# Three attention stages of a two-block transformer: the search for row maxima spread over more steps, the softmax sums taken as columns, the division moved behind the transposition, one more addition per block on GpSimd

## The chip, the cores and the metric

One NeuronCore of a Trainium2 chip runs the whole program. The time is device microseconds from start to end of one execution; the runs of the kernel before have a median of 5038.33 us (5033.85 to 5042.69, three runs). Engines are named as the profile names them: PE is TensorE, PEld its weight load, DVE VectorE, ACT ScalarE, POOL GpSimd, SP SyncE; a "q" behind a name is the engine's queue (its semaphore and DMA instructions).

## The reference, cut to what matters

Two transformer blocks on 1024 tokens of width 1024: an MLA plus dilated attention block with 16 experts, then two layers that each have three kinds of attention on 1024 tokens plus 256 context tokens. The change touches those attentions that see every key:

```python
def mla_attention(q, k, v):                       # first block, 8 heads, 1024 keys
    s = jnp.einsum('bqhd,bkhd->bhqk', q_blk, k).astype(jnp.float32) * scale
    p = jax.nn.softmax(s, axis=-1).astype(v.dtype)
    return jnp.einsum('bhqk,bkhd->bqhd', p, v)

def diff_attend(q, k, v, lam):                    # each layer of the second, 8 maps, 1280 keys
    s = jnp.einsum('bqhmd,bkhmd->bhmqk', q, k).astype(jnp.float32) * (q.shape[-1] ** -0.5)
    p = jax.nn.softmax(s, axis=-1)

def gqa_attend(q, k, v):                          # each layer of the second, 6 heads, 1280 keys
    s = jnp.einsum('bqhgd,bkhd->bhgqk', qg, k).astype(jnp.float32) * (d ** -0.5)
    p = jax.nn.softmax(s, axis=-1).astype(v.dtype)
    o = jnp.einsum('bhgqk,bkhd->bqhgd', p, v)
```

So each needs, for every query, the maximum of its scores, the exponentials, their sum, their product with v, and a division.

## The kernel before, in words

All five such attentions go through one function, `stage_turned`: `am` (MLA, 8 heads in 4 pairs, 1024 keys), and in each of two layers `aa` (8 maps in 4 pairs, 1280 keys) and `ab` (6 heads in 3 pairs, 1280 keys). The profile writes no layer number, so `aa` and `ab` stand for both layers; the time tells them apart (layer 0 from 2560 us, layer 1 from 4110 us).

A pair of heads is cut in *blocks* of 512 queries (two in each pair; layer 0 has a third, small one of 256 context queries against 256 keys). A block is walked in *steps* of 128 keys, numbered i in the block and g in the stage: 8 steps in `am`, 10 in `aa` and `ab`, 2 in the small block. In a step

- PE (`scores`) multiplies 128 keys by 512 queries for both heads into the scores' PSUM buffers `sp`, two in turn; the scores come out turned, with keys on the partitions. A score takes one pass for a head in `aa`, two in `ab`, three in `am`.
- ACT (`exponentials`) writes exp of both heads, 128x1024, into a ring `pT` of six. The maximum is subtracted inside the matmul: a row of the operand `qA` (`qB` in `ab`) holds the negated maxima.
- PE (`values`), in odd steps only, multiplies two earlier steps' exponentials by v into `po`, eight passes of 512 columns in all.
- For the sums, the exponentials are added over the steps: DVE adds steps 0 and 1 and the block's last one into `accd`, POOL the steps between into `accp`, and DVE adds the two (L1535, L1540, POOL L1587).

The maxima of a block must be known before its first step, so they are *searched* while the block ahead of it runs. A *piece* is a matmul of 128 queries by up to 512 keys (`search`, L1396) into one of two PSUM buffers `mp`, and a DVE reduction of it to one column (L1519). A block has 16 pieces in `am` (2 heads x 4 tiles x 2), and 24 in `aa` and `ab` (2 x 4 x 3; of three pieces one is 256 wide). Each piece waits until the one two before it is reduced (semaphore `mc`). PE and DVE take them in the same order, four to a step: steps 0 to 3 in `am`, 0 to 5 in `aa` and `ab` (0 to 6 in a first block of layer 0, which also searches for the small one).

When all are reduced, `row` turns the maxima on PE (L1404), ACT copies them (L1478), and SP writes them to memory and reads them back as a row of the next block's operand (L1362, L1366); the next block's first scores wait for that (semaphore `rw`). It stands two steps behind the last searched one.

Behind a block's end, counted in steps from its last: 4 steps later PE sums over the partitions with a matrix of ones (`sums`, L1437, out 64x512 for each head) into a buffer of `mp`, in turn with the pieces; DVE takes the reciprocal of 128x512 (L1546) and multiplies `po` by it (L1551). 6 steps later PE turns the result (`turned`, L1446), behind the values, into a buffer of `sp`; ACT copies it out (L1495) and POOL stores it.

Every engine runs its own list in program order, with no reordering: an engine that waits for one semaphore holds up all that stands behind it. Inside one step DVE's list is: the pieces of the step, then `add(g - 2)`, then the normalisation; PE's is: scores, pieces, in odd steps sums and values, then `turned`, then `row`.

## Time and profile before

| | |
|---|---|
| median of the runs shown | 5038.33 us (5033.85 to 5042.69) |
| profiled execution, its own time | 5035.54 us |
| its span, from the first to the last instruction | 5033.9 us |
| granted TensorE clock over the span | 0.851 |
| the five stages (507 to 787, 2560 to 2890, 2935 to 3195, 4110 to 4425, 4460 to 4700 us) | 1425 us in all |

What lies around the span is 1.6 us, so times inside the span add straight to the time. The granted clock is 1.00 at 2.4 GHz and 0.50 at 1.2 GHz; a figure between is a mean over a stretch.

### The profile page before, as it was taken

Reading aid. Unit: us, or ns where it says so; the run is one execution under the profiler, and the core shown is the slowest. Engines: PE = TensorE matmul, PEld = TensorE weight load, DVE = VectorE, ACT = ScalarE, POOL = GpSimd, SP = SyncE. Lnnn points to the kernel's source line nnn. Section 1 sums busy time; section 2 is a strip of 40 time slices with the busy share of each in tenths; the row PEclk is TensorE's granted clock in tenths of the full one; section 3 lists DMA queues with packets and bytes.
Section 4 is the critical chain, followed back from the end, with each engine's and each line's share of the span. In section 5 each row is a group of like instructions: output and inputs, shape, how many; then the busy total and the mean of one; then the engine's idle time right before and its main releaser. Section 6 shows DMA issues by size and latency. Waiting matters only on the chain. (4 is left out here: it accounts for less than half of the span.)

```text
span 5033.9 us, 55601 instructions
## 1 busy us (share of the span) xinstructions
PE 3815.4 (76%) x18714; PEld 2694.3 (54%) x18714; DVE 2606.4 (52%) x4549; ACT 1773.2 (35%) x2670; POOL 1407.2 (28%) x974
## 2 busy tenths in 40 slices
PE   3985886886299995589968868576688978858557
PEld 3973444665278884477833334355576753324346
DVE  2114453432678786744445546466556535545465
ACT  1225224731077774422212312354422212312352
POOL 0213231000056662144613413200044613423102
PEclk6997798997699997799967868888799977868798
DMA  5228213316699994322232032423222331131333
GB/s 210 97 107 243 66 38 72 102 47 237 167 396 398 394 394 175 102 88 92 97 90 52 9 77 47 92 82 109 81 97 76 102 78 59 26 71 40 88 105 90
DMA packets 327678, 628.00 MB, mean 125 GB/s; under 512 B 115338, under 2 KB 171892, under 8 KB 326364
## 3 DMA queue, kind: packets, MB, share of 16 engines
q1 hardware_dynamic: 289080, 494.92, 31.4%
q0 software_dynamic: 34240, 113.67, 7.1%
q10 hardware_dynamic: 4068, 15.79, 0.8%
q8 instruction: 152, 2.49, 0.2%
q14 instruction: 138, 1.13, 0.1%
HBM read 485.18 MB, written 139.11 MB: 124 GB/s over the span
## 5 line engine op out<-in xcount | busy, mean ns | idle before, releaser
L2282 PE MATMUL pr_ps<-pr_wH,hT_part 128*128 128x512 f32 x1120 | 447.5, 400 | 0.0
L2052 ACT ACTIVATE ex_high<-ex_ring 128x2048 fp32r<-128x2048 f32 x192 | 368.7, 1920 | 96.0 <-PE ex_pg L2028 37.6
L2098 DVE TENSOR_TENSOR ex_ring_part<-ex_ring,ex_high 128x2048 fp32r<-128x2048 f32 x144 | 371.8, 2582 | 50.7 <-ACTq L2053 38.8
L2282 PE MATMUL pr_ps<-pr_wH,x_sb_part 128*128 128x512 f32 x896 | 366.2, 409 | 22.8 <-DVEq L2355 22.8
L2282 PE MATMUL pr_ps<-pr_w_part,x_sb_part 128*128 128x512 f32 x896 | 358.9, 401 | 0.0
L1519 DVE TENSOR_REDUCE aa_part<-aa_mp 128x1 f32<-128x512 f32 (+1 forms) x400 | 238.1, 595 | 207.1 <-PE aa_mp L1396 171.8
L1993 POOL TENSOR_TENSOR ex_ring_part<-ex_ring,ex_high 128x2048 fp32r<-128x2048 f32 x48 | 239.4, 4988 | 215.3 <-ACTq L2053 215.3
L1396 PE MATMUL aa_mp<-aa_kA,aa_qA 96*128 96x512 f32 (+1 forms) x400 | 199.0, 538 | 120.9 <-DVEq L1520 73.7
L1487 ACT ACTIVATE aa_pT<-aa_sp 128x1024 f32<-128x1024 f32 (+1 forms) x168 | 168.6, 1003 | 313.1 <-PE aa_sp L1417 304.1
L1519 DVE TENSOR_REDUCE ab_part<-ab_mp 128x1 f32<-128x512 f32 (+1 forms) x300 | 178.7, 596 | 182.8 <-PE ab_mp L1396 155.6
L2282 PEld LDWEIGHTS pr_ps<-pr_wH,hT_part 128*128 128x128 f32 x1120 | 217.2, 194 | 47.5
L2428 POOL TENSOR_TENSOR pr_w_part<-pr_w,pr_wH 128x512 fp32r<-128x512 f32 x96 | 124.4, 1296 | 406.8 <-ACTq L2308 405.2
L1396 PE MATMUL ab_mp<-ab_kA,ab_qA 128*128 128x512 f32 (+1 forms) x300 | 141.9, 515 | 120.1 <-DMA ab_v<-proj 57.1
L1658 PE MATMUL o_ps<-o_wH,o_yT 128*128 128x512 f32 x832 | 231.5, 396 | 0.0
L1587 POOL TENSOR_TENSOR aa_accp<-aa_accp,aa_pT 128x1024 f32<-128x1024 f32 x80 | 194.3, 2429 | 94.0 <-ACTq L1488 91.1
L1487 ACT ACTIVATE ab_pT<-ab_sp 128x1024 f32<-128x1024 f32 (+1 forms) x126 | 126.4, 1003 | 255.2 <-PE ab_sp L1417 250.8
L1396 PEld LDWEIGHTS aa_mp<-aa_kA,aa_qA 96*128 96x128 f32 x400 | 94.0, 236 | 226.2 <-DVEq L1520 170.5
L1428 PE MATMUL aa_po<-aa_pT,aa_v 128*64 128x512 f32 x672 | 213.2, 769 | 0.0
L2282 PEld LDWEIGHTS pr_ps<-pr_wH,x_sb_part 128*128 128x128 f32 x896 | 175.3, 196 | 58.5 <-issue 23.4
L2368 DVE TENSOR_REDUCE pr_ss<-pr_sqr 128x8 f32<-128x512 f32 (+2 forms) x80 | 49.6, 619 | 287.8 <-ACTq L2331 284.1
L1045 PE MATMUL ac_ps<-ac_kT,ac_qT 128*128 128x384 f32 (+1 forms) x204 | 75.4, 374 | 155.8 <-DVEq L1111 84.2
L2282 PEld LDWEIGHTS pr_ps<-pr_w_part,x_sb_part 128*128 128x128 f32 x896 | 174.7, 195 | 34.9
(387 smaller groups left out, 9026.5 us busy)
## 6 DMA issues: line engine op xcount, KB each, us to landing
ex_ring<-in_w_gate SPq DMA_DIRECT2D x64, 1024.0 KB, 9.6
ex_ring<-in_w_up SPq DMA_DIRECT2D x64, 1024.0 KB, 8.1
ex_ring<-in_w_down SPq DMA_DIRECT2D x64, 1024.0 KB, 7.9
z_d<-pr_zT POOLq DMA_DIRECT2D x120, 256.0 KB, 3.0
rt_mw<-in_w_ada SPq DMA_DIRECT2D x14, 2048.0 KB, 15.6
pr_w<-in_w_in SPq DMA_DIRECT2D x14, 2048.0 KB, 8.5
mod_w<-in_w_ada SPq DMA_DIRECT2D x10, 2048.0 KB, 13.1
proj<-pr_raw POOLq DMA_DIRECT2D x60, 256.0 KB, 2.3
```

The costliest lines, as they stand in the source:

```text
L1045: mm = tensor.matmul(ps[h % SB][:, at:at + m], q.bitcast(F32R), kk.bitcast(F32R), start=i == 0, stop=i == len(ab) - 1)
L1396: tensor.matmul(mp[:, k_ % 2, 0:w], qA[rows, b, j, q0:q0 + P].bitcast(F32R), kA[rows, b, j, a_:a_ + w].bitcast(F32R), start=True, stop=Tru ...
L1428: mm = tensor.matmul(po[j * dv:(j + 1) * dv, B % 2, 0:qn], v[:, p % 2, k0 // P + i, j * dv:(j + 1) * dv], pT[:, g % RP, j, 0:qn], start=i ...
L1487: scalar.activation(pT[:, g % RP, :, 0:qn], sp_[:, s % 2, :, 0:qn], ACT.Exp)
L1519: vector.tensor_reduce(part[:, B % 2, j * n + t, x:x + 1], mp[:, k_ % 2, 0:w], AX.X, ALU.max)
L1587: pool.tensor_tensor(acc, pT[:, (g - 3) % RP, :, 0:qn] if i == 3 else acc, pT[:, (g - 2) % RP, :, 0:qn], ALU.add).then_inc(ap_, 1)
L1658: mm = tensor.matmul(ps[:, t % 2, cols], yT[:, t % 2, part, c, :].bitcast(F32R), w[:, c, cols].bitcast(F32R), start=c == 0 and i == 0, sto ...
L1993: pool.tensor_tensor(w_part[:, c % SL].bitcast(F32R), w_sb[:, c % SL], wH[:, c % HL], ALU.subtract)\
L2052: scalar.activation(wH[:, c % HL].bitcast(F32R), w_sb[:, c % SL], ACT.Copy)
L2098: vector.tensor_tensor(w_part[:, c % SL].bitcast(F32R), w_sb[:, c % SL], wH[:, c % HL], ALU.subtract)
L2282: mm = tensor.matmul(ps[:, g % 4, :], x.bitcast(F32R), w[:, c % 2, kk, :].bitcast(F32R), start=kk == 0 and i == 0, stop=kk == KC - 1 and i ...
L2428: pool.tensor_tensor(w_part[w].bitcast(F32R), w_sb[w], wH[w], ALU.subtract).then_inc(w_low, 1)
```

## The change

The search of a block is spread evenly over all but the last two steps of the block ahead of it (`searched`): 3 pieces in each of 8 steps in layer 1 (4 and 3 in turn in a first block of layer 0), and 3, 3, 2, 3, 3, 2 in `am`. The row of maxima comes one step behind the last searched step instead of two (`row_at`).

POOL adds every step from the third to the last; DVE adds only the first two and then the two sums. DVE's additions stand three steps behind instead of two (`add(g - 3)`).

The sums come out as columns: `sums` uses 128 columns of `accd` as weights and one column of ones as the moving operand, eight matmuls for a block of 512 queries, and leaves 128x8 in `mp`. DVE takes the reciprocal of these eight columns. ACT copies `po` to `oT` undivided (`gathered`, 3 steps behind the end). PE turns it into a buffer of `mp` instead of one of `sp`, ahead of the values, and DVE divides while it copies out (`divided`). `slot_out` and `slot_den` now both count places among the pieces.

```diff
@@ -1235,26 +1235,22 @@
             p, B, blk, i = where(g)
             if size[blk] <= 2:
                 return []
-            ahead = [B + 1] if blk + 1 < NB and size[blk + 1] > 2 else [b for b in (B + 1, B + 2) if b % NB == 0 or size[b % NB] <= 2]
-            if blk == 0 and NB == 3:
-                ahead = [B + 1, B + 2]
-            if blk == 1 and NB == 3:
-                ahead = [B + 2]
+            ahead = [B + 1] if NB == 2 else [B + 1, B + 2] if blk == 0 else [B + 2]
             pcs = [(b, m) for b in ahead if b < NBLK for m in range(len(maxima(b)))]
-            return pcs[4 * i:4 * i + 4]
+            n = size[blk] - 2
+            return pcs[-(-len(pcs) * i // n):-(-len(pcs) * (i + 1) // n)] if i < n else []
 
         def row_at(B):
 
             if B == 0:
                 return -1
-            return 2 + max(g for g in range(TOT) if any(b == B for b, _ in searched(g)))
+            return 1 + max(g for g in range(TOT) if any(b == B for b, _ in searched(g)))
...
-        D_AT, F_AT, S_AT = 4, 6, 8
-        out_at = {end(B) + F_AT: B for B in range(NBLK)}
+        O_AT, D_AT, F_AT, S_AT = 3, 4, 6, 8
...
         def on_dve(blk, i):
-            return size[blk] <= 2 or i in (0, 1, size[blk] - 1)
+            return i < 2
...
@@ -1433,37 +1429,39 @@
                     qn, k_ = blocks[B % NB][1], slot_den(B)
                     pe.wait_ge(ac, B + 1)
                     pe.wait_ge(mc, k_ - 1)
-                    for j in range(2):
-                        mm = tensor.matmul(mp[j * dv:(j + 1) * dv, k_ % 2, 0:qn], ones[:, j * dv:(j + 1) * dv],
-                                           accd[:, B % 2, j, 0:qn], start=True, stop=True)
+                    for t in range(qn // P):
+                        for j in range(2):
+                            mm = tensor.matmul(mp[:, k_ % 2, 2 * t + j:2 * t + j + 1], accd[:, B % 2, j, t * P:(t + 1) * P],
+                                               ones[:, 0:1], start=True, stop=True)
                     mm.then_inc(mf, 1)
 
                 def turned(B):
-                    s = slot_out(B)
+                    k_ = slot_out(B)
                     pe.wait_ge(nr, B + 1)
-                    pe.wait_ge(sr, s - 1)
+                    pe.wait_ge(mc, k_ - 1)
                     for t in range(tiles_of(B)):
-                        mm = tensor.transpose(sp_[:, s % 2, 0, t * P:(t + 1) * P], oT[:, B % 2, t * P:(t + 1) * P], ident[:, :])
-                    mm.then_inc(st, 1)
+                        mm = tensor.transpose(mp[:, k_ % 2, t * P:(t + 1) * P], oT[:, B % 2, t * P:(t + 1) * P], ident[:, :])
+                    mm.then_inc(mf, 1)
 
                 pe.wait_ge(ones_in, 1)
                 for m in range(len(maxima(0))):
                     search(0, m, m)
                 row(0)
-                for g in range(TOT + F_AT):
+                for g in range(TOT + F_AT + 1):
                     if g < TOT:
                         scores(g)
                         for x, (B, m) in enumerate(searched(g)):
                             search(B, m, pieces_before[g] + x)
+                    for B in range(NBLK):
+                        if end(B) + D_AT == g:
+                            sums(B)
+                    for B in range(NBLK):
+                        if end(B) + F_AT == g:
+                            turned(B)
                     if g % 2:
-                        for B in range(NBLK):
-                            if end(B) + D_AT == g:
-                                sums(B)
                         for x in (g - 3, g - 2):
                             if 0 <= x < TOT:
                                 values(x)
-                    if g in out_at:
-                        turned(out_at[g])
                     for B in range(1, NBLK):
                         if rows_at[B] == g:
                             row(B)
@@ -1487,20 +1485,21 @@
                     scalar.activation(pT[:, g % RP, :, 0:qn], sp_[:, s % 2, :, 0:qn], ACT.Exp)
                     act.drain().then_inc(sr, 1)
 
-                def finished(B):
-                    s, n = slot_out(B), tiles_of(B)
-                    act.wait_ge(st, s + 1)
+                def gathered(B):
+                    qn = blocks[B % NB][1]
+                    act.wait_ge(pv, end(B) + 1)
                     if B >= 2:
-                        act.wait_ge(os_[B % 2], 16 * (B // 2))
-                    scalar.activation(o[:, B % 2, 0:n, :], sp_[:, s % 2, 0, 0:n * P].rearrange("p (t d) -> p t d", d=P), ACT.Copy)
-                    act.drain().then_inc(sr, 1)
+                        act.wait_ge(mf, slot_out(B - 2) + 1)
+                    scalar.activation(oT[:, B % 2, 0:qn], po[:, B % 2, 0:qn], ACT.Copy)
+                    act.drain().then_inc(nr, 1)
 
                 row(0)
-                for g in range(TOT + F_AT):
+                for g in range(TOT + F_AT + 1):
                     if g < TOT:
                         exponentials(g)
-                    if g in out_at:
-                        finished(out_at[g])
+                    for B in range(NBLK):
+                        if end(B) + O_AT == g:
+                            gathered(B)
                     for B in range(1, NBLK):
                         if rows_at[B] == g:
                             row(B)
@@ -1528,28 +1527,35 @@
                 def add(g):
                     p, B, blk, i = where(g)
                     qn, n = blocks[blk][1], size[blk]
+                    if i == n - 1 and n > 2:
+                        last = added(g)
+                        dve.wait_ge(*last)
+                        vector.tensor_tensor(accd[:, B % 2, :, 0:qn], accd[:, B % 2, :, 0:qn], accp[:, B % 2, :, 0:qn], ALU.add)
+                        dve.drain().then_inc(ac, 1)
                     if not on_dve(blk, i) or i == 0:
                         return
                     acc = accd[:, B % 2, :, 0:qn]
                     dve.wait_ge(sr, slot_scores(g) + 1)
                     vector.tensor_tensor(acc, pT[:, (g - 1) % RP, :, 0:qn] if i == 1 else acc, pT[:, g % RP, :, 0:qn], ALU.add)
                     dve.drain().then_inc(ad, 1)
-                    if i == n - 1:
-                        if n > 2:
-                            dve.wait_ge(ap_, p * pool_adds[NSTEP] + pool_adds[g % NSTEP])
-                            vector.tensor_tensor(acc, acc, accp[:, B % 2, :, 0:qn], ALU.add)
+                    if n == 2:
                         dve.drain().then_inc(ac, 1)
 
-                def normalised(B):
-                    qn, k_ = blocks[B % NB][1], slot_den(B)
+                def sums(B):
+                    n, k_ = 2 * tiles_of(B), slot_den(B)
                     dve.wait_ge(mf, k_ + 1)
-                    vector.reciprocal(rB[:, 0:qn], mp[:, k_ % 2, 0:qn])
+                    vector.reciprocal(rd[:, B % 2, 0:n], mp[:, k_ % 2, 0:n])
                     dve.drain().then_inc(mc, 1)
-                    dve.wait_ge(pv, end(B) + 1)
+
+                def divided(B):
+                    n, k_ = 2 * tiles_of(B), slot_out(B)
+                    dve.wait_ge(mf, k_ + 1)
                     if B >= 2:
-                        dve.wait_ge(st, slot_out(B - 2) + 1)
-                    vector.tensor_tensor(oT[:, B % 2, 0:qn], po[:, B % 2, 0:qn], rB[:, 0:qn], ALU.mult)
-                    dve.drain().then_inc(nr, 1)
+                        dve.wait_ge(os_[B % 2], 16 * (B // 2))
+                    vector.tensor_tensor(o[:, B % 2, 0:n // 2, :].rearrange("p t (j d) -> p (t j) d", d=dv),
+                                         mp[:, k_ % 2, 0:n * dv].rearrange("p (c d) -> p c d", d=dv),
+                                         rd[:, B % 2, 0:n].rearrange("p (c o) -> p c o", o=1).to_broadcast([P, n, dv]), ALU.mult)
+                    dve.drain().then_inc(mc, 1)
...
@@ -1561,15 +1567,18 @@
                 dve.drain().then_inc(ones_in, 1)
                 for m in range(len(maxima(0))):
                     search(0, m, m)
-                for g in range(TOT + F_AT):
+                for g in range(TOT + F_AT + 1):
                     if g < TOT:
                         for x, (B, m) in enumerate(searched(g)):
                             search(B, m, pieces_before[g] + x)
-                    if 0 <= g - 2 < TOT:
-                        add(g - 2)
+                    if 0 <= g - 3 < TOT:
+                        add(g - 3)
                     for B in range(NBLK):
                         if end(B) + D_AT == g:
-                            normalised(B)
+                            sums(B)
+                    for B in range(NBLK):
+                        if end(B) + F_AT == g:
+                            divided(B)
 
             @block.gpsimd
             def _(pool):
...
-                            pool.wait_ge(sr, slot_out(B) + 1)
+                            pool.wait_ge(mc, slot_out(B) + 1)
```

Three places in the engines' lists, from one block in the middle of stage `aa`, second layer. First DVE. Before, one block of ten steps; the x8 are the pieces of two steps, `nm` is the final maximum:

```order
L1519 TENSOR_REDUCE aa_part<-aa_mp 128x1 x8
L1535 TENSOR_TENSOR aa_accd<-aa_accd,aa_pT 128x1024
L1540 TENSOR_TENSOR aa_accd<-aa_accd,aa_accp 128x1024
L1519 TENSOR_REDUCE aa_part<-aa_mp 128x1 x8
L1535 TENSOR_TENSOR aa_accd<-aa_pT 128x1024
L1546 RECIPROCAL aa_rB<-aa_mp 128x512
L1551 TENSOR_TENSOR aa_oT<-aa_po,aa_rB 128x512
L1519 TENSOR_REDUCE aa_part<-aa_mp 128x1 x8
L1524 TENSOR_REDUCE aa_nm<-aa_part 128x8
```

The same block now:

```order
L1518 TENSOR_REDUCE aa_part<-aa_mp 128x1 x9
L1533 TENSOR_TENSOR aa_accd<-aa_accd,aa_accp 128x1024
L1518 TENSOR_REDUCE aa_part<-aa_mp 128x1 x3
L1547 RECIPROCAL aa_rd<-aa_mp 128x8
L1518 TENSOR_REDUCE aa_part<-aa_mp 128x1 x3
L1539 TENSOR_TENSOR aa_accd<-aa_pT 128x1024
L1518 TENSOR_REDUCE aa_part<-aa_mp 128x1 x3
L1555 TENSOR_TENSOR aa_o<-aa_mp,aa_rd 128x512
L1518 TENSOR_REDUCE aa_part<-aa_mp 128x1 x6
L1523 TENSOR_REDUCE aa_nm<-aa_part 128x8
```

Before, both additions stood behind the pieces of an odd step. Now each stands behind the pieces of an even step (i = 2 and i = 4), ahead of those of the odd step that follows.

Second PE, steps 3 to 5 of the block (`mp` from `kA` is a piece, `po` the values). Before:

```order
L1437 MATMUL aa_mp<-aa_accd,aa_one 64x512 x2
L1428 MATMUL aa_po<-aa_pT,aa_v 64x512 x4
L1417 MATMUL aa_sp<-aa_qA,aa_kA 128x512 x2
L1396 MATMUL aa_mp<-aa_kA,aa_qA 128x512
L1396 MATMUL aa_mp<-aa_kA,aa_qA 128x256
L1396 MATMUL aa_mp<-aa_kA,aa_qA 128x512 x2
L1417 MATMUL aa_sp<-aa_qA,aa_kA 128x512 x2
L1396 MATMUL aa_mp<-aa_kA,aa_qA 128x256
L1396 MATMUL aa_mp<-aa_kA,aa_qA 128x512 x2
L1396 MATMUL aa_mp<-aa_kA,aa_qA 128x256
L1428 MATMUL aa_po<-aa_pT,aa_v 64x512 x4
L1446 MATMUL aa_sp<-ident,aa_oT 128x128 x4
```

Now:

```order
L1434 MATMUL aa_mp<-aa_one,aa_accd 128x1 x8
L1424 MATMUL aa_po<-aa_pT,aa_v 64x512 x4
L1413 MATMUL aa_sp<-aa_qA,aa_kA 128x512 x2
L1392 MATMUL aa_mp<-aa_kA,aa_qA 128x512 x2
L1392 MATMUL aa_mp<-aa_kA,aa_qA 128x256
L1413 MATMUL aa_sp<-aa_qA,aa_kA 128x512 x2
L1392 MATMUL aa_mp<-aa_kA,aa_qA 128x512 x2
L1392 MATMUL aa_mp<-aa_kA,aa_qA 128x256
L1443 MATMUL aa_mp<-ident,aa_oT 128x128 x4
L1424 MATMUL aa_po<-aa_pT,aa_v 64x512 x4
```

Six pieces instead of eight stand between two groups of values, the turning moved ahead of the values and into `mp`, and the sums are eight matmuls of one column.

Third PE, the last steps of the block (the `nm` row is `row`, and the block's last values come just ahead of the next block's scores). Before:

```order
L1417 MATMUL aa_sp<-aa_qA,aa_kA 128x512 x4
L1428 MATMUL aa_po<-aa_pT,aa_v 64x512 x4
L1404 MATMUL aa_sp<-ident,aa_nm 8x128
L1417 MATMUL aa_sp<-aa_qA,aa_kA 128x512 x4
L1428 MATMUL aa_po<-aa_pT,aa_v 64x512 x4
```

Now:

```order
L1424 MATMUL aa_po<-aa_pT,aa_v 64x512 x4
L1413 MATMUL aa_sp<-aa_qA,aa_kA 128x512 x2
L1400 MATMUL aa_sp<-ident,aa_nm 8x128
L1413 MATMUL aa_sp<-aa_qA,aa_kA 128x512 x2
L1424 MATMUL aa_po<-aa_pT,aa_v 64x512 x4
```

The row of maxima moved one step nearer to the scores that wait for it, from ahead of step 8's scores to behind them.

## Rows read from the trace of the kernel before

**Rows 1.** The page: busy us of each engine, share of the span, instructions.

```profile
PE 3815.4 (76%) x18714; PEld 2694.3 (54%) x18714; DVE 2606.4 (52%) x4549; ACT 1773.2 (35%) x2670; POOL 1407.2 (28%) x974
```

**Rows 2.** Windows: length, busy of PE, PEld, DVE, ACT, POOL; clock, DMA share, GB/s.

```profile
563.10:758.20 195.10, 167.02 (x631) 87.98 (x630) 116.01 (x134) 54.34 (x61) 60.91 (x30) 0.97 0.20 47
4166.70:4394.50 227.80, 195.62 (x559) 76.50 (x559) 135.55 (x181) 66.60 (x73) 87.80 (x42) 0.79 0.13 29
4511.50:4667.60 156.10, 134.36 (x454) 63.97 (x453) 90.84 (x121) 44.41 (x49) 59.82 (x29) 0.87 0.16 34
2614.80:2862.80 248.00, 206.55 (x628) 85.28 (x628) 150.97 (x205) 72.14 (x85) 94.28 (x45) 0.78 0.13 30
2991.80:3161.10 169.30, 140.18 (x507) 69.05 (x506) 105.02 (x138) 48.05 (x57) 61.15 (x30) 0.89 0.16 36
```

**Rows 3.** PE's waits, 4110 to 4425: us in total, times, longest.

```profile
PE aa_mp L1396 <- DVEq L1520: 31.0, 70, 1.3
```

**Rows 4.** Timeline of steps 0 and 1 of an `aa` block, layer 1.

```profile
4281.31 0.73 PE L1417 MATMUL aa_sp<-aa_qA,aa_kA 97*128 97x512 f32 x2 [0.59 <-DMA aa_qA<-aa_nmd]
...
4282.32 5.82 DVE L1519 TENSOR_REDUCE aa_part<-aa_mp 128x1 f32<-128x512 f32 x8 [10.90 <-PE aa_mp L1396]
4283.09 0.39 PE L1396 MATMUL aa_mp<-aa_kA,aa_qA 96*128 96x256 f32 x1 [0.58 <-DVEq L1520]
...
4287.21 3.39 PE L1428 MATMUL aa_po<-aa_pT,aa_v 128*64 128x512 f32 x8
...
4290.53 0.73 PE L1417 MATMUL aa_sp<-aa_qA,aa_kA 97*128 97x512 f32 x2
```

**Rows 5.** Windows of 3.4 us in these steps (columns as in Rows 2).

```profile
4283.40:4286.80 3.40, 2.37 (x8) 1.24 (x7) 2.81 (x6) 1.02 (x1) 0.08 (x1) 0.99 0.00 0
4286.80:4290.20 3.40, 3.40 (x9) 0.76 (x8) 3.04 (x4) 0.00 (x0) 0.00 (x0) 0.50 0.01 2
```

**Rows 6.** Groups of DVE instructions by form, 4110 to 4425.

```profile
L1519 DVE TENSOR_REDUCE aa_part<-aa_mp 128x1 f32<-128x512 f32 x124 | 85.7, 692 | 97.2 <-PE aa_mp L1396 86.8
L1546 DVE RECIPROCAL aa_rB<-aa_mp 128x512 f32<-128x512 f32 x8 | 26.9, 3357 | 2.9 <-PE aa_mp L1437 2.1
L1519 DVE TENSOR_REDUCE aa_part<-aa_mp 128x1 f32<-128x256 f32 x62 | 26.3, 424 | 11.5 <-PE aa_mp L1396 5.5
```

**Rows 7.** Timeline: a block's first scores and first reduction, `am` then `ab`.

```profile
659.85 0.50 PE L1417 MATMUL am_sp<-am_qA,am_kA 97*128 97x512 f32 x1
...
661.78 1.50 DVE L1519 TENSOR_REDUCE am_part<-am_mp 128x1 f32<-128x512 f32 x2 [10.83 <-PE am_mp L1396]
...
4550.75 0.50 PE L1417 MATMUL ab_sp<-ab_qA,ab_kA 128*128 128x512 f32 x1
...
4552.23 0.69 DVE L1519 TENSOR_REDUCE ab_part<-ab_mp 128x1 f32<-128x512 f32 x1 [12.63 <-PE ab_mp L1396]
```

**Rows 8.** Timeline of steps 7 to 9 of the `aa` block and the next's start.

```profile
4313.17 1.94 PE L1428 MATMUL aa_po<-aa_pT,aa_v 128*64 128x512 f32 x8
...
4315.03 0.27 PE L1404 MATMUL aa_sp<-ident,aa_nm 128*8 128x128 f32 x1
...
4315.35 0.27 ACT L1478 ACTIVATE aa_nmT<-aa_sp 8x128 fp32r<-8x128 f32 x1 [0.51 <-PE aa_sp L1404]
...
4315.81 1.02 ACT L1487 ACTIVATE aa_pT<-aa_sp 128x1024 f32<-128x1024 f32 x1 [0.20 <-PE aa_sp L1417]
...
4318.72 0.73 PE L1417 MATMUL aa_sp<-aa_qA,aa_kA 97*128 97x512 f32 x2 [0.43 <-DMA aa_qA<-aa_nmd]
```

**Rows 9.** Timeline: VectorE's addition while GpSimd adds, end of `am`.

```profile
754.53 2.36 POOL L1587 TENSOR_TENSOR am_accp<-am_accp,am_pT 128x1024 f32<-128x1024 f32 x1 [0.73 <-ACTq L1488]
...
755.82 2.16 DVE L1535 TENSOR_TENSOR am_accd<-am_accd,am_pT 128x1024 f32<-128x1024 f32 x1 [6.52 <-ACTq L1488]
```

**Rows 10.** Timeline: the next addition, with GpSimd idle.

```profile
758.09 1.23 DVE L1540 TENSOR_TENSOR am_accd<-am_accd,am_accp 128x1024 f32<-128x1024 f32 x1
```

**Rows 11.** Timeline: sixteen passes of 128x128 weights and 16 columns (router).

```profile
1206.29 1.96 PE L1855 MATMUL rt_lp<-rt_wr,rt_hT 128*128 128x16 f32 x16
```

**Rows 12.** Groups by form, 1500 to 2600: a product from PSUM with a broadcast.

```profile
L2383 DVE TENSOR_TENSOR pr_z<-pr_ps,pr_r 128x512 f32<-128x512 f32 x30 | 20.8, 692 | 2.2
```

15 lines of the change are left out of this document (7 added, 8 removed).

## Prediction

> **What bounds the kernel now.** The page first [rows 1]: PE is busy 76% of the span, DVE 52%, and no other engine comes near. All that changes lies in the five `stage_turned` stages, some 1425 us, so I read windows over their steady blocks [rows 2]. They hold six `am` blocks in 195.1 us (32.5 each), six `aa` blocks of layer 1 in 227.8 (38.0), four `ab` blocks of layer 1 in 156.1 (39.0), and in layer 0 six large and three small `aa` blocks in 248.0 and four large and two small `ab` blocks in 169.3. The reader is to see two things: DVE is busy only 58 to 62% of these stretches, so it is no bound by its sum, and the granted clock is 0.97 in `am`, 0.87 to 0.89 in `ab`, 0.78 to 0.79 in `aa`.
>
> The view of waits says what ties PE up [rows 3]: in `aa`, layer 1, it waits 31.0 us in 70 places for DVE's queue behind a reduction. The timeline shows how [rows 4]. Scores start at 4281.31 and the first reduction 1.01 us later. Eight reductions run in 5.82 us. Each 512-wide one is 0.692 and each 256-wide one 0.424 [rows 6], so with some 0.12 of handling the pitch is 0.81 and 0.55 (six and two of these make 5.96, less the last handling). With two buffers, piece n's matmul waits for the reduction of piece n-2; so the values start at 4287.21, when six reductions are over. From this I take one formula for a pair of steps (an even one, and an odd one with its values): time to the first reduction, plus all reductions but the last two, plus 0.4 for the last matmul, plus the values, 1.9 at full clock [rows 8]. For the pair in [rows 4] it gives 1.0 + 4.3 + 0.4 = 5.7 to the values, seen 5.9.
>
> The second thing in [rows 4] is the clock. The values take 3.39 us there and 1.94 in [rows 8]. The windows say why [rows 5]: from 4283.4 to 4286.8 PE waits between pieces at a granted clock of 0.99, and the next stretch, in which the values run, is granted 0.50, the 1.2 GHz level. So a pause in the search is paid twice: 1.45 us more for the values behind it.
>
> **The change part by part.** All at full clock first.
>
> *Spreading.* Layer 1: four pairs of six pieces instead of three of eight. A plain pair of six in `aa` is 1.0 + 3.0 + 0.4 + 1.9 = 6.3. In `ab` the first reduction comes at 1.5 [rows 7] and the second scores delay one by 0.1: 6.9. In `am` it comes at 1.9 [rows 7], all pieces are 512 wide and the second scores cost 0.4: 7.9. For a block this saves little, since every pair pays the start and the values anyway: three pairs of eight and two bare ones against four of six and one bare.
>
> *The additions.* This is where I expect the loss. Until now both stood behind an odd step's pieces, covered by the values. Now the merging addition stands behind step 2's pieces and the other behind step 4's, with an odd step's pieces queued behind them, and PE's piece matmuls, sums or turning, and values behind those. An addition is 1.23 [rows 10], 1.35 with handling, and the formula puts all of it on the path. The one in step 4 meets GpSimd: exp of step 4 ends some 1.9 us after the pair's start, GpSimd adds it until about 4.4, and VectorE wants to start at 3.2. In [rows 9] such an addition, begun 1.07 before GpSimd's ended, took 2.16. Bounds: 1.35 if they pass each other, 3.6 if it waits for a whole 2.36. I take 2.25 in `aa`, 2.1 in `ab`, 1.8 in `am`.
>
> *Sums.* Two matmuls of 512 columns become eight with 128x128 weights and one column. The trace has no such matmul; the nearest are sixteen passes with 16 columns in 1.96 us, the last one's run-out included, 0.11 to 0.12 each [rows 11]. Float32 products run in two passes here (values: eight passes for four matmuls), so 16 of them make 1.8 us. They wait for the last piece but one, one reduction more than the last piece's matmul: 0.8. Bounds: nothing to 3.6 (half clock).
>
> *Turning.* Four passes, 0.45, ahead of the values and with the same extra reduction, 0.8. Before, it cost ACT's copy ahead of the next scores.
>
> *Reciprocal and division.* 3.36 us [rows 6] become a reciprocal of eight columns, some 0.2, and the product from PSUM with a broadcast is 0.69 [rows 12], as the multiplication was. It is hidden before by the values and bare steps, all but about 1 us in `aa`; now it is hidden behind the values.
>
> *The row of maxima.* In [rows 8] the copy of the row starts at 4315.35 and the scores that wait for it at 4318.72: 3.4 us. Turned behind step 8's scores, the copy queues behind that step's exp (0.8 to 1.9), so the next block can start at 1.9 + 3.4 = 5.3 instead of 3.7. In `ab` 5.7 instead of 3.9, in `am` 6.3 instead of 4.9. In layer 0 the small block's two steps cover it, but step 9's scores still wait for the exp: 4.4 and 5.0.
>
> *Hidden:* ACT's copy of `po` (ACT is busy under a third) and GpSimd's seventh addition (2.4 us in blocks of 38, where it is busy 15; with that cover gone, at a stage's end, it delays the last block by about what the shorter reciprocal gives back).
>
> *Blocks.* `aa`, layer 1: 6.3 + (6.3 + 1.35 + 0.8 + 1.8) + (6.3 + 2.25 + 0.8 + 0.45) + 6.3 + 5.3 = 38.0, against 38.0. `ab`, layer 1: 6.9 + 10.85 + 10.25 + 6.9 + 5.7 = 40.6, against 39.0. `am` (pieces 3+3, 2+3, 3+2): 7.9 + 10.4 + 9.7 + 6.3 = 34.3, against 32.5. Layer 0, first blocks with seven pieces in a pair and two sums (`aa`): 11.05 + 10.1 + 10.4 + 7.1 + 4.4 = 43.05, second 6.3 + 10.25 + 9.8 + 6.3 + 4.4 = 37.05, the small one left at its 2.8, so the stretch is 3 x 43.05 + 3 x 37.05 + 3 x 2.8 = 248.7 against 248.0. `ab` the same way: 2 x 46.1 + 2 x 39.9 + 2 x 3.5 (small ones as before) = 179.0 against 169.3. Differences: 0, 4 x 1.6, 6 x 1.8, 0.7, 9.7: **+28 us** at full clock.
>
> *Clock.* The old blocks have their low clock in these numbers, the new ones do not yet. In every pair with an addition ahead of sums or turning PE now stands still for some 3 to 4 us, with one or two pieces in it; that is emptier than the stretch in [rows 5], which had the lower level behind it. There are 2 such pairs in a block of layer 1 and `am` (12 + 12 + 8), 15 in layer 0's `aa` and 10 in its `ab`: 57. At 1.45 each, +83 us.
>
> The sum is +111 us on the profiled execution's 5035.5, so 5146, which I round to **5145 us**; that execution lies 2.8 us under the median of the runs. A difference under 0.2% (10 us) can't be told from none.
>
> **The rivals.**
>
> *The clock stays up.* The waits are spread, no stretch is as empty as I think, and the old low clock was due to eight pieces in a row. Then only the +28 stays: 5063. For it: `am` keeps 0.97 with 60% of DVE's time in use. Against it: [rows 5]. The Trainium skill ("TensorE: Matmul & The Clock Gate", Loop structure matters more than you think) speaks for it: VectorE copying a result out of PSUM between groups of matmuls does not cool PE, which only long waits for transfers do. By that rule the sum would be 5063; no row here has PE resting that short without the lower level behind it in `aa`, so the trace speaks against it.
>
> *Faster: the additions cost nothing.* If VectorE's work behind an even step's pieces falls where PE has scores to do, the additions and the extra reduction drop out: 5.2 us in each `aa` block, 5.05 in `ab`, 4.7 in `am`, 6.8 and 6.65 in the first blocks of layer 0, together 6 x 5.2 + 4 x 5.05 + 6 x 4.7 + 3 x 12.0 + 2 x 11.7 = 139 us, and the low clock with them: 5063 - 139 = 4924. For it: DVE rests some 40% of the time, and 2.7 us of it are freed in a block. It decides from the point where a fifth of these waits vanishes, if the clock stays up, and four fifths if it doesn't. Against it: the two buffers leave PE only two pieces of lead.
>
> *Worse clock.* Sums run at the lower level too (28 of 1.8 us, +50) and half of the plain pairs' values (some 20 at 1.45, +29): 5225.
>
> *No change.* The order shifts waits about and losses equal gains: 5035 to 5045.
>
> **How the numbers follow.** Sum as worked out 0.47, worse clock 0.13, clock stays up 0.18, faster 0.17, no change 0.05. Low end 5040, between no change and the full clock case; high end 5225, the worse clock: this leaves out the faster case and little else. The likeliest case's own range is 5100 to 5190. Slower 0.78, same 0.05, faster 0.17.
>
> **What would show it.** Right: in `aa`, layer 1, blocks of 40 us or more; PE's first long wait of a block in front of step 3's last piece and the column sums, with VectorE in the merging addition; additions of step 4 over 2 us; sixteen passes of sums in 1.8 us or 3.6; values over 3 us behind both; a wait of 1.5 us for the row at a block's start; a lower mean clock in `am` than 0.97. Wrong: values of 1.9 us behind the sums, or the merging addition finished before step 3's scores are. If GpSimd's last addition came late, the merging addition would wait and hold all pieces behind it, which I have at nothing.

## The result, and the profile after

| | before | after |
|---|---|---|
| median (lowest to highest, runs) | 5036.09 us (5030.64 to 5042.69, 4) | 5207.21 us (5200.00 to 5212.28, 4) |
| ratio, 95% interval | 1 | 1.0338 (1.0320 to 1.0356) |
| profiled execution, its span | 5035.54, 5033.9 us | 5200.00, 5198.4 us |
| granted clock over the span | 0.851 | 0.846 |

The change makes the kernel 171 us slower between the medians, 164.5 between the profiled executions. The page's first line answers to [rows 1]; below it stand two of its groups (busy, mean ns of one, idle time ahead of it and what ended most of that):

```profile
PE 3894.0 (75%) x19174; PEld 2789.4 (54%) x19174; DVE 2451.6 (47%) x4513; ACT 1773.1 (34%) x2670; POOL 1512.5 (29%) x1010
...
L1518 DVE TENSOR_REDUCE aa_part<-aa_mp 128x1 f32<-128x512 f32 (+1 forms) x400 | 238.2, 596 | 332.8 <-PE aa_mp L1392 295.1
...
L1392 PE MATMUL aa_mp<-aa_kA,aa_qA 96*128 96x512 f32 (+1 forms) x400 | 185.3, 500 | 157.0 <-DVEq L1519 110.1
```

DVE does 155 us less work than before and POOL 105 more, and both are busy for less than half of the span; PE's matmuls are busy 79 us longer. Windows over the same steady blocks as in [rows 2], in the same order and with the same columns, show that the whole loss lies there (164 of the 164.5 us):

```profile
551.50:779.10 227.60, 185.03 (x703) 105.55 (x702) 92.16 (x126) 54.30 (x60) 77.84 (x36) 0.90 0.16 40
4258.50:4525.30 266.80, 205.11 (x632) 91.20 (x630) 113.98 (x174) 66.60 (x73) 110.84 (x49) 0.80 0.11 25
4649.20:4830.40 181.20, 140.61 (x501) 73.66 (x500) 76.06 (x116) 44.40 (x49) 72.53 (x33) 0.87 0.13 30
2632.00:2922.40 290.40, 233.26 (x712) 109.33 (x711) 122.15 (x198) 72.11 (x84) 111.97 (x52) 0.74 0.11 26
3054.80:3249.10 194.30, 156.21 (x563) 83.42 (x562) 81.32 (x132) 48.06 (x56) 73.29 (x35) 0.83 0.13 31
```

They are 32.5, 39.0, 25.1, 42.4 and 25.0 us longer, 164 together. The mean clock hardly shows it in layer 1 (0.79 and 0.80 in `aa`, 0.87 and 0.87 in `ab`), since the stretches themselves have grown. A block is now 37.9 us in `am` (32.5 before), 44.5 in `aa` and 45.3 in `ab`, layer 1 (38.0 and 39.0). PE's time outside its matmuls went from 28.1 to 42.6 us in `am` and from 32.2 to 61.7 in `aa`, layer 1.

The timeline of one `aa` block, layer 1, steps 0 to 5 (start, duration, and in brackets the idle time ahead and what ended it), shows all of it at once:

```profile
4347.00 0.73 PE L1413 MATMUL aa_sp<-aa_qA,aa_kA 97*128 97x512 f32 x2 [0.86 <-DMA aa_qA<-aa_nmd]
...
4348.01 4.21 DVE L1518 TENSOR_REDUCE aa_part<-aa_mp 128x1 f32<-128x512 f32 x6 [8.24 <-PE aa_mp L1392]
...
4351.26 3.23 PE L1424 MATMUL aa_po<-aa_pT,aa_v 128*64 128x512 f32 x8
...
4357.34 1.05 PE L1392 MATMUL aa_mp<-aa_kA,aa_qA 96*128 96x512 f32 x2
...
4357.92 1.23 DVE L1533 TENSOR_TENSOR aa_accd<-aa_accd,aa_accp 128x1024 f32<-128x1024 f32 x1
...
4359.26 2.04 DVE L1518 TENSOR_REDUCE aa_part<-aa_mp 128x1 f32<-128x512 f32 x3
4360.04 0.29 PEld L1392 LDWEIGHTS aa_mp<-aa_kA,aa_qA 96*128 96x128 f32 x1 [1.97 <-DVEq L1519]
4360.04 0.58 PE L1392 MATMUL aa_mp<-aa_kA,aa_qA 96*128 96x256 f32 x1 [1.65 <-DVEq L1519]
...
4360.94 3.54 PE L1434 MATMUL aa_mp<-aa_one,aa_accd 128*128 128x1 f32 x16 [0.32 <-DVEq L1519]
...
4364.42 3.68 PE L1424 MATMUL aa_po<-aa_pT,aa_v 128*64 128x512 f32 x8
...
4370.34 5.66 POOL L1596 TENSOR_TENSOR aa_accp<-aa_accp,aa_pT 128x1024 f32<-128x1024 f32 x2 [8.99 <-ACTq L1486]
...
4371.55 2.25 DVE L1539 TENSOR_TENSOR aa_accd<-aa_pT 128x1024 f32<-128x1024 f32 x1
4373.91 2.05 DVE L1518 TENSOR_REDUCE aa_part<-aa_mp 128x1 f32<-128x512 f32 x3
...
4374.69 0.58 PE L1392 MATMUL aa_mp<-aa_kA,aa_qA 96*128 96x256 f32 x1 [2.67 <-DVEq L1519]
...
4375.59 1.09 PE L1443 MATMUL aa_mp<-ident,aa_oT 128*128 128x128 f32 x4 [0.32 <-DVEq L1519]
```

Step 3's first two piece matmuls are done at 4358.4. Their reductions could have begun at once; VectorE is in the merging addition until 4359.15. So the third piece waits 1.65 us, the sums wait for one reduction more, and in the 2.5 us up to the sums PE is busy for 0.6. Windows of 3.4 us (columns as in [rows 2]) give the clock for it:

```profile
4354.40:4357.80 3.40, 2.82 (x10) 1.57 (x8) 1.81 (x3) 1.94 (x3) 0.00 (x0) 0.89 0.00 0
4357.80:4361.20 3.40, 1.38 (x5) 0.76 (x4) 2.93 (x4) 0.70 (x1) 2.53 (x1) 0.62 0.00 0
4361.20:4364.60 3.40, 3.40 (x18) 3.38 (x19) 0.18 (x2) 0.00 (x0) 0.14 (x1) 0.50 0.00 0
4364.60:4368.00 3.40, 3.40 (x8) 0.58 (x6) 0.13 (x1) 0.00 (x0) 0.00 (x0) 0.50 0.00 0
4368.00:4371.40 3.40, 2.82 (x10) 1.59 (x8) 1.78 (x3) 1.37 (x2) 1.06 (x1) 0.88 0.00 0
```

PE is busy 1.38 of 3.4 us in the third of them, and the two stretches behind it are granted 0.50 throughout: first the sums run in them (3.54 us for sixteen passes), then the values (3.68). Cut where the level changes, the same trace reads

```profile
4355.20:4358.50 3.30, 2.57 (x9) 1.07 (x7) 2.39 (x4) 2.64 (x3) 0.00 (x0) 1.00 0.00 0
4358.60:4368.80 10.20, 8.44 (x27) 5.22 (x28) 2.56 (x5) 0.00 (x0) 2.68 (x1) 0.50 0.00 0
4368.90:4372.20 3.30, 2.49 (x8) 1.00 (x7) 2.46 (x4) 2.05 (x2) 1.86 (x1) 1.00 0.00 0
```

So in this block the level falls 0.2 us after the wait has begun and returns only behind the values, 10.2 us later. In 25 of the 26 large blocks of the five stretches the clock is at 1.00 when PE begins this wait, and it falls within 4.8 us. The forecast had the lower level for the values alone. In step 5 VectorE's other addition takes 2.25 us beside GpSimd's, and PE waits 2.67 us.

The view of waits for 4200 to 4560 us (us in total, times, longest) answers to [rows 3]; PE waits for the reductions as often as it did, 70 times, but 53.1 us instead of 31.0:

```profile
PE aa_mp L1392 <- DVEq L1519: 53.1, 70, 2.7
PE aa_sp L1413 <- DMA aa_qA<-aa_nmd: 10.1, 8, 3.5
```

### The profile page after: what moved, and what is told of

Same layout as the page of the kernel before. It is cut to its first block and busy times, and to the rows that moved or that the text cites. A ratio compares the mean times of both kernels' runs of the same rounds, so it can differ in the third digit from the quotient of the medians.

```text
span 5198.4 us, 56521 instructions
## 1 busy us (share of the span) xinstructions
PE 3894.0 (75%) x19174; PEld 2789.4 (54%) x19174; DVE 2451.6 (47%) x4513; ACT 1773.1 (34%) x2670; POOL 1512.5 (29%) x1010
## 3 DMA queue, kind: packets, MB, share of 16 engines
q1 hardware_dynamic: 289080, 494.92, 30.4%
## 5 line engine op out<-in xcount | busy, mean ns | idle before, releaser
L1392 PE MATMUL aa_mp<-aa_kA,aa_qA 96*128 96x512 f32 (+1 forms) x400 | 185.3, 500 | 157.0 <-DVEq L1519 110.1
L1596 POOL TENSOR_TENSOR aa_accp<-aa_accp,aa_pT 128x1024 f32<-128x1024 f32 x96 | 238.5, 2485 | 192.2 <-ACTq L1486 188.4
L1392 PE MATMUL ab_mp<-ab_kA,ab_qA 128*128 128x512 f32 (+1 forms) x300 | 127.0, 480 | 137.7 <-DVEq L1519 81.2
L1424 PE MATMUL aa_po<-aa_pT,aa_v 128*64 128x512 f32 x672 | 227.2, 814 | 0.0
L1596 POOL TENSOR_TENSOR ab_accp<-ab_accp,ab_pT 128x1024 f32<-128x1024 f32 x72 | 177.8, 2470 | 141.8 <-ACTq L1486 139.3
## 6 DMA issues: line engine op xcount, KB each, us to landing
mod_w<-in_w_ada SPq DMA_DIRECT2D x10, 2048.0 KB, 12.9
```

Of the source, the lines that this page charges most:

```text
L1392: tensor.matmul(mp[:, k_ % 2, 0:w], qA[rows, b, j, q0:q0 + P].bitcast(F32R), kA[rows, b, j, a_:a_ + w].bitcast(F32R), start=True, stop=Tru ...
L1424: mm = tensor.matmul(po[j * dv:(j + 1) * dv, B % 2, 0:qn], v[:, p % 2, k0 // P + i, j * dv:(j + 1) * dv], pT[:, g % RP, j, 0:qn], start=i ...
L1596: pool.tensor_tensor(acc, pT[:, (g - 3) % RP, :, 0:qn] if i == 3 else acc, pT[:, (g - 2) % RP, :, 0:qn], ALU.add).then_inc(ap_, 1)
```

## The experiments

Times are medians; each is compared with runs of the kernel before on the same chip (5033.4 to 5037.2 us) and has the interval of that ratio. To see in which pair of steps a kernel spends its time, this table has the mean distance between the starts of ACT's exponentials of steps 0, 2, 4, 6 and 8 in each kernel's profiled execution, over the steady blocks:

| kernel | `am`: block, pairs | `aa`, layer 1 | `ab`, layer 1 |
|---|---|---|---|
| before | 32.5: 9.9 11.6 6.2 4.9 | 38.0: 9.6 10.4 11.0 3.2 3.7 | 39.0: 8.4 12.1 10.6 4.0 3.9 |
| forecast at full clock | 34.3: 7.9 10.4 9.7 6.3 | 38.0: 6.3 10.25 9.8 6.3 5.3 | 40.6: 6.9 10.85 10.25 6.9 5.7 |
| after | 37.9: 8.0 13.1 10.5 6.3 | 44.5: 7.1 13.1 11.8 7.0 5.4 | 45.3: 6.8 13.8 12.0 6.8 5.9 |
| e1_spread | 35.3: 8.7 8.2 11.6 6.8 | 41.1: 8.1 8.9 11.3 7.4 5.4 | 41.1: 6.8 8.7 12.8 6.8 6.0 |
| e2_pool | 33.9: 9.6 13.1 6.2 5.0 | 41.2: 10.1 11.3 12.9 3.2 3.7 | 40.6: 8.4 11.9 12.4 4.0 3.9 |
| e3_columns | 34.1: 9.6 14.4 5.3 4.9 | 40.8: 10.0 13.1 11.0 3.1 3.6 | 40.7: 8.4 14.1 10.3 3.9 3.9 |
| e4_odd_adds | 33.5: 7.9 11.1 8.2 6.4 | 39.1: 7.7 11.2 8.4 6.4 5.3 | 38.7: 6.8 11.2 8.0 6.8 5.9 |
| e5_sums_behind | 33.7: 7.9 9.8 9.5 6.4 | 42.5: 8.5 11.3 11.1 6.2 5.4 | 40.9: 6.8 9.7 11.7 6.8 5.8 |
| e6_odd_behind | 30.7: 7.9 8.8 7.6 6.3 | 36.8: 7.4 9.0 8.8 6.2 5.4 | 37.0: 6.8 8.6 8.9 6.8 5.9 |
| e7_row_late | 34.1: 9.6 12.2 5.3 7.1 | 40.4: 9.9 10.9 11.0 3.2 5.4 | 42.6: 9.6 9.6 13.6 4.0 5.8 |
| e8_row_early | 31.6: 8.8 9.8 8.2 4.9 | 38.4: 9.6 10.6 9.9 4.6 3.7 | 36.5: 7.8 9.0 10.4 5.4 3.9 |
| e9_wide_sums | 37.5: 7.9 13.4 9.8 6.3 | 44.5: 7.4 13.3 11.6 6.7 5.5 | 45.4: 6.8 13.9 12.0 6.8 5.9 |
| e10_packed | 31.9: 9.6 11.6 5.9 4.9 | 40.7: 9.6 13.3 11.0 3.1 3.6 | 35.7: 8.4 9.9 9.5 3.9 3.9 |
| e11_early_wide | 30.3: 8.8 9.7 6.9 4.9 | 35.2: 9.2 9.1 8.6 4.5 3.7 | 33.8: 7.8 9.0 7.6 5.4 4.0 |
| e12_dve_last | 30.4: 8.8 9.8 6.9 4.9 | 37.8: 9.4 10.2 9.9 4.6 3.7 | 34.1: 7.8 9.3 7.6 5.4 3.9 |

My theory, C in the expectations: the additions between an even and an odd step's pieces and the lower clock behind these stalls together make the loss. Its rivals: A, the additions carry nearly all of it and the column sums nothing; S, spreading the search is itself what costs.

### The three parts alone, e1 to e3

**e1_spread** is the kernel before with the new search and the row one step behind it (VectorE's additions stay at `g - 2`):

```diff
-            return pcs[4 * i:4 * i + 4]
+            n = size[blk] - 2
+            return pcs[-(-len(pcs) * i // n):-(-len(pcs) * (i + 1) // n)] if i < n else []
...
-            return 2 + max(g for g in range(TOT) if any(b == B for b, _ in searched(g)))
+            return 1 + max(g for g in range(TOT) if any(b == B for b, _ in searched(g)))
```

> The kernel before with one part of the change: the search spread over all but the last two steps of a block, the row of maxima one step behind it. Theory C (columns): the loss comes from sixteen weight loads with one column ahead of the values, which run with PE nearly empty and keep the granted clock at its lower level; then this part costs only the later row, 1.5 us in each of some 19 blocks of layer 1 and of the first attention, less about 1 us saved in each pair's start: 0 to +30 us on the kernel before. Theory A (additions): the same small figure. Theory S (spreading): four pairs with values at the lower clock instead of three are the loss: +80 us or more.

Measured: 5069.36 us, 1.0054 (1.0037 to 1.0072), so +32 us, just above the 0 to 30 of A and C. S falls. The first three pairs together are shorter in `aa` (28.3 against 31.0), and the last two pay it back (12.8 against 6.9): each now has six pieces or the late row.

**e2_pool** is the kernel before with GpSimd adding the last step and VectorE's additions one step later:

```diff
         def on_dve(blk, i):
-            return size[blk] <= 2 or i in (0, 1, size[blk] - 1)
+            return i < 2
...
-                    if 0 <= g - 2 < TOT:
-                        add(g - 2)
+                    if 0 <= g - 3 < TOT:
+                        add(g - 3)
```

> The kernel before with one part of the change: GpSimd adds the last step too, VectorE's additions three steps behind instead of two, so they stand behind even steps. Theory A: the additions in the middle of a pair are the loss, 1.35 + 2.25 us in each of 31 blocks and the lower clock behind them: +100 to +150 us. Theory C: 40 to 70 us, since the old sums do not wait long behind them. Theory S: 0 to +30 us.

Measured: 5120.36 us, 1.0167 (1.0150 to 1.0184), +83 us: between C's 40 to 70 and A's 100 to 150, so neither number holds. The groups of VectorE's additions in `aa`, layer 1 (4211.8 to 4459.1 us), say what these 83 us are not:

```profile
L1540 DVE TENSOR_TENSOR aa_accd<-aa_pT 128x1024 f32<-128x1024 f32 x6 | 7.4, 1226 | 0.7
L1534 DVE TENSOR_TENSOR aa_accd<-aa_accd,aa_accp 128x1024 f32<-128x1024 f32 x6 | 7.4, 1226 | 0.7
```

Neither addition meets GpSimd here (1226 ns each), and there is one addition per block less on VectorE. What is left is their place: pieces queue behind them. That is an inference here; e4 tests it.

**e3_columns** is the kernel after with the old search, row and additions, so it has the column sums, ACT's copy, the turning in `mp` and the late division:

```diff
-                        mm = tensor.matmul(mp[j * dv:(j + 1) * dv, k_ % 2, 0:qn], ones[:, j * dv:(j + 1) * dv],
-                                           accd[:, B % 2, j, 0:qn], start=True, stop=True)
+                            mm = tensor.matmul(mp[:, k_ % 2, 2 * t + j:2 * t + j + 1], accd[:, B % 2, j, t * P:(t + 1) * P],
+                                               ones[:, 0:1], start=True, stop=True)
```

> The kernel before with one part of the change: sums as columns, the division on the turned output, turning into the search's buffers. Theory C: sums of 1.8 to 3.5 us instead of 0.9 to 1.1, the values behind them at the lower clock in every block, less about 1 us for the shorter reciprocal: +50 to +100 us. Theory A: within 20 us of the kernel before. Theory S: the same.

Measured: 5082.06 us, 1.0093 (1.0076 to 1.0110), +45 us. A's number (within 20) falls, and C's is just missed from below. In the table the second pair, the one with the sums, grows by 2.0 to 2.8 us and no other by more than 0.4. PE's groups of sums and values there (4189.2 to 4434.0 us):

```profile
L1427 PE MATMUL aa_po<-aa_pT,aa_v 128*64 128x512 f32 x240 | 88.5, 878 | 0.0
...
L1437 PE MATMUL aa_mp<-aa_one,aa_accd 128*128 128x1 f32 x96 | 20.0, 338 | 0.3
```

Six groups of sixteen passes in 20.0 us are 3.3 us each, the lower level's price, though there is no addition ahead of them: eight pieces in a row bring it as well.

The parts alone make 32 + 83 + 45 = 160 us, the whole 171. They nearly add up.

### Undone in the changed kernel, e4 to e6

**e4_odd_adds** is the kernel after with VectorE's additions back at `g - 2`, so that they stand behind an odd step's pieces:

```diff
-                    if 0 <= g - 3 < TOT:
-                        add(g - 3)
+                    if 0 <= g - 2 < TOT:
+                        add(g - 2)
```

> The changed kernel with VectorE's additions two steps behind again, so that the merging one stands behind step 1 and the other behind step 3, in front of the values. Theory A: nearly all of the loss goes, 120 to 170 us below the changed kernel. Theory C: only the additions' own time goes, 60 to 100 us below it, and the values behind the column sums still take over 3 us. Theory S: less than 50 us below it.

Measured: 5043.04 us (5011.19 to 5059.36 in ten runs), 1.0003 (0.9985 to 1.0021). One step's place is worth 164 us, all but 7 of the loss. A's number holds and C's was too small. Pairs two and three get 1.9 to 4.0 us shorter each. The clock is still low behind many sums: they take 15.7 us for six in `aa`, layer 1 (20.1 after), and the values behind them there still 3.5 to 3.7 us each, as C had it.

**e5_sums_behind** is the kernel after with sums and turning behind the odd step's values:

```diff
+                    if g % 2:
+                        for x in (g - 3, g - 2):
+                            if 0 <= x < TOT:
+                                values(x)
                     for B in range(NBLK):
                         if end(B) + D_AT == g:
                             sums(B)
...
-                    if g % 2:
-                        for x in (g - 3, g - 2):
-                            if 0 <= x < TOT:
-                                values(x)
```

> The changed kernel with the column sums and the turning behind the values of their odd step instead of ahead. Clock theory: the sixteen weight loads hold PE at the lower level, and the values behind them pay it; with the values first, these bring the clock up and the sums run in 1.8 us instead of 3.5. Then the pair with the sums falls from 13.1 to 10.5 or less in each stage (1.8 us of sums, 0.8 of waiting for one more reduction), the one with the turning by 1, together 80 to 110 us below the changed kernel. Rival, order without clock: each group keeps its duration and only the waiting of 0.8 us in two pairs of a block goes: 40 to 50 us below it, sums still 3.5 us.

Measured: 5123.25 us, 1.0173 (1.0158 to 1.0188), 84 us below the kernel after and inside the clock theory's 80 to 110; the rival, in which only the wait for the extra reduction goes, had 40 to 50. In `am` and `ab` the sums now take 11.7 us for six and 7.8 for four, 1.95 each, and their pair is down to 9.8 and 9.7. In `aa` the theory's detail missed: the sums still take 2.8 us each (16.6 for six), and their pair 11.3 instead of 10.5 or less.

**e6_odd_behind** is the kernel after with both of these edits, e4's and e5's.

> The changed kernel with both: VectorE's additions two steps behind (as in e4_odd_adds) and sums and turning behind the values. Clock theory: the pair with the sums falls from 11.2 to some 9, that with the turning from 8.2 by 0.5 to 1: 50 to 80 us below e4_odd_adds, 4960 to 4990 us, faster than the kernel before. Rival, order without clock: 20 to 40 us below e4_odd_adds, 5005 to 5020 us.

Measured: 4993.42 us (4981.57 to 4997.82), 0.9910 (0.9897 to 0.9923): faster than the kernel before by 41 us, 214 us below the kernel after, and 50 below e4. That is 3 us above the clock theory's numbers (4960 to 4990) and clear of the rival's (5005 to 5020); the pair with the sums fell to 8.6 to 9.0, as the theory had it. Its timeline at a block's steps 3 to 5 in `aa`, layer 1, against the one above:

```profile
4225.35 3.30 PE L1424 MATMUL aa_po<-aa_pT,aa_v 128*64 128x512 f32 x8
4226.22 2.01 DVE L1539 TENSOR_TENSOR aa_accd<-aa_pT 128x1024 f32<-128x1024 f32 x1
4228.58 1.95 PE L1434 MATMUL aa_mp<-aa_one,aa_accd 128*128 128x1 f32 x16
4230.39 0.71 PE L1413 MATMUL aa_sp<-aa_qA,aa_kA 97*128 97x512 f32 x2
```

The addition that meets GpSimd (2.01 us) lies inside the values and holds nothing up; the sums wait for nothing and take 1.95 us. The windows of the same stretches as above (`am`, then `aa` and `ab` of layer 1):

```profile
557.70:741.60 183.90, 163.85 (x703) 96.28 (x702) 92.56 (x127) 54.28 (x61) 75.74 (x37) 0.98 0.20 49
4143.30:4364.20 220.90, 187.47 (x631) 80.49 (x631) 112.45 (x174) 66.59 (x73) 103.27 (x48) 0.84 0.13 30
4484.20:4632.10 147.90, 124.62 (x501) 66.24 (x501) 75.84 (x116) 44.40 (x48) 69.20 (x33) 0.94 0.17 36
```

### The row, the spreading and the last addition: e7, e8, e10, e12

**e7_row_late** is the kernel before with the row one step later:

```diff
-            return 2 + max(g for g in range(TOT) if any(b == B for b, _ in searched(g)))
+            return 3 + max(g for g in range(TOT) if any(b == B for b, _ in searched(g)))
```

> The kernel before with nothing changed but the row of maxima one step later. If the later row is what costs at a block's end, the last pair of a block grows from 4.9 to 6.3 in the first attention, from 3.7 to 5.3 and from 3.9 to 5.8 in layer 1, in 19 blocks: +30 us, plus up to 10 in layer 0 where the next scores wait for the exponentials. If instead the last piece's reduction or the pieces themselves made those pairs longer in the changed kernel, this stays within 10 us of the kernel before.

Measured: 5086.78 us, 1.0096 (1.0081 to 1.0111), +52 us where 30 to 40 were expected. The last pairs go from 4.9 to 7.1, 3.7 to 5.4 and 3.9 to 5.8, as the forecast's 3.4 us from copy to scores has it in `aa` and `ab`. In `am` the last pair was forecast at 6.3. Alone the late row costs more than the whole of e1, so the spread search itself should give back about 20 (52 less 32); that is a difference of two runs, not a run of its own, and in the first blocks of layer 0 the row does not stand in the same step in both.

**e8_row_early** is e6 with the search ending one step earlier, which brings the row forward too:

```diff
-            n = size[blk] - 2
+            n = size[blk] - 3
```

> e6_odd_behind with the search spread over all but the last three steps, so the row of maxima stands behind the values of the last but two as before. A block's last pair falls by 1.4 to 1.9 us in 19 blocks of layer 1 and the first attention, the pairs ahead of it get one more piece, 0.7 us each, of which the last but one loses three: 10 to 30 us below e6_odd_behind. If pieces left alone in the pair ahead cost as much as six, no gain.

Measured: 4984.35 us (4973.00 to 5005.22), 0.9900 (0.9880 to 0.9921), 9 us below e6, where 10 to 30 were expected; single runs of the two overlap, so the gain is hardly clear of noise. The last pairs are back at 4.9, 3.7 and 3.9, and the table shows the first three pairs of a block longer in every stage: the pieces moved ahead eat most of it.

**e10_packed** is e6 with the old search and row:

```diff
-            return pcs[-(-len(pcs) * i // n):-(-len(pcs) * (i + 1) // n)] if i < n else []
+            return pcs[4 * i:4 * i + 4]
...
-            return 1 + max(g for g in range(TOT) if any(b == B for b, _ in searched(g)))
+            return 2 + max(g for g in range(TOT) if any(b == B for b, _ in searched(g)))
```

> e6_odd_behind with the search as before the change, four pieces in a step and the row of maxima two steps behind the last. If spreading the search is worth something once additions and sums stand well, this is slower than e6_odd_behind by 10 us or more (5005 or above). If it is worth nothing and costs the later row, this is 20 to 40 us faster than e6_odd_behind, 4955 to 4975.

Measured: 5041.25 us (5026.60 to 5048.32, twelve runs), 1.0011 (1.0000 to 1.0022). So with additions and sums well placed, the spread search, its late row included, is worth 48 us (5041.25 to 4993.42), where 10 or more were expected; put alone into the kernel before it costs 32.

**e12_dve_last** is e8 with VectorE adding a block's last step again, ahead of the merging addition:

```diff
-            return i < 2
+            return size[blk] <= 2 or i in (0, 1, size[blk] - 1)
```

> e8_row_early with the block's last step added by VectorE again, as before the change. VectorE's 1.35 us stand behind step 1's pieces, under the values: if these cover them, within 10 us of e8_row_early; if they reach into step 2's pieces, 1.35 us in up to 31 blocks, 15 to 40 us above it.

Measured: 4975.99 us, 0.9888 (0.9867 to 0.9908), 8 us below e8. That is inside the "within 10 us" expected if the values cover the addition. GpSimd's seventh addition gives nothing.

### Are the sums' few columns to blame? e9 and e11

Behind the sums the clock stayed low. K says that it does because sixteen passes of one column are hardly work; W says that the wait ahead of them decides, whatever their columns. **e9_wide_sums** is the kernel after with 64 columns in each of these matmuls instead of one; the reciprocal reads the first of each 64:

```diff
-                            mm = tensor.matmul(mp[:, k_ % 2, 2 * t + j:2 * t + j + 1], accd[:, B % 2, j, t * P:(t + 1) * P],
-                                               ones[:, 0:1], start=True, stop=True)
+                            c = (2 * t + j) * dv
+                            mm = tensor.matmul(mp[:, k_ % 2, c:c + dv], accd[:, B % 2, j, t * P:(t + 1) * P],
+                                               ones[:, 0:dv], start=True, stop=True)
```

> The changed kernel with 64 columns of ones as moving operand of the column sums instead of one: sixteen passes with the same weight loads, 64 times the columns, no more time for it at either level, the first column of each group read by the reciprocal. Theory K: it is the one-column passes that keep the granted clock at its lower level through the sums and the values behind them; filled with columns they let it rise, the values behind the sums go from 3.6 us to about 2 and the pair with the sums from 13.1 by 1.5 to 2.5: 40 to 70 us below the changed kernel. Theory W: the wait ahead of the sums decides the clock for all that follows, and the sums' columns nothing: within 10 us of the changed kernel.

Measured: 5192.32 us, 1.0316 (1.0295 to 1.0337), 15 us below the kernel after: just past W's 10, far from K's 40 to 70, and its interval overlaps that of the kernel after (1.0320 to 1.0356). **e11_early_wide** is the same edit in e8, where the sums stand behind the values.

> e8_row_early with the 64-column sums of e9_wide_sums. Theory K: the sums there follow the values, so only the pair behind them gains, up to 1 us in a block: 0 to 30 us below e8_row_early. Theory W: within 10 us of it.

Measured: 4944.51 us (4936.60 to 4951.28), 0.9816 (0.9799 to 0.9832), the fastest of all; 40 us below e8, more than K's 30 and W's 10, so neither theory foresaw it. Groups of sums and values in `aa`, layer 1, of the kernel after, then of e9, then of e11:

```profile
L1424 PE MATMUL aa_po<-aa_pT,aa_v 128*64 128x512 f32 x240 | 86.0, 856 | 0.0
...
L1434 PE MATMUL aa_mp<-aa_one,aa_accd 128*128 128x1 f32 x96 | 20.1, 340 | 2.9 <-DVEq L1519 2.9
```

```profile
L1424 PE MATMUL aa_po<-aa_pT,aa_v 128*64 128x512 f32 x240 | 85.6, 853 | 0.0
...
L1435 PE MATMUL aa_mp<-aa_one,aa_accd 128*128 128x64 f32 x96 | 20.6, 404 | 2.7 <-DVEq L1520 2.7
```

```profile
L1424 PE MATMUL aa_po<-aa_pT,aa_v 128*64 128x512 f32 x240 | 78.8, 792 | 0.0
...
L1435 PE MATMUL aa_mp<-aa_one,aa_accd 128*128 128x64 f32 x96 | 12.0, 278 | 0.0
```

In `aa`, columns behind a wait change nothing (340 and 404 ns, both some 3.4 us for sixteen passes, and values of 2.9 us a pair on average). In `am` the values get 4.4 us shorter (59.4 to 55.0) and the sums 3.9 longer (18.0 to 21.9). That the columns are what makes e11 faster is less sure than its time. Its `am` and `ab` run at a granted clock of 1.00, but so do those of e12, with one column:

```profile
4444.70:4580.00 135.30, 118.03 (x501) 63.41 (x500) 76.14 (x116) 44.42 (x48) 69.43 (x33) 1.00 0.18 40
```

```profile
4470.30:4606.70 136.40, 118.09 (x501) 63.40 (x500) 82.40 (x121) 44.36 (x48) 59.85 (x28) 1.00 0.19 39
```

These are four `ab` blocks of layer 1 in e11 (first) and e12; e8 has 146.1 us at 0.89 for them. What e11 has over e12 (31 us) lies in `aa` of layer 1 (211.0 against 226.7 us) and `ab` of layer 0 (147.0 against 162.9). Whether columns or a shift of a fraction of a microsecond between stalls brought that, these runs don't tell apart.

## Why the prediction was right, and where its sum was short

**Sign and mechanism: right, and shown.** Sequence in the trace: merging addition, PE's wait at step 3's last piece, sums, values over 3 us, as forecast; the second addition at 2.25 us, the value taken for `aa` (on average 2.23 there, 2.00 in `am` where 1.8 was taken); a clock in `am` of 0.90 instead of 0.97. Moving the additions back by one step (e4) takes 164 us off. The forecast had 89.7 for them at full clock (21.6 + 13.8 + 18.9 + 21.6 + 13.8 over the five stretches) and 83 of low clock behind them, 173 in all.

**In size: inside the range, but above what the likeliest case allowed.** 5207 lies within 5040 to 5225 only because the high end was put at the rival "worse clock"; the likeliest case had given itself 5100 to 5190.

**The part at full clock, +28: about right.** The pairs that the clock spares fit it closely: `am` 8.0 and 6.3 (7.9 and 6.3 forecast), `ab` 6.8, 6.8 and 5.9 (6.9, 6.9, 5.7), `aa` 5.4 (5.3). The row of maxima costs what was said.

**The clock, +83: too small, and this is the term that was mis-sized.** It can be read from the groups of values, sums and turning in the five stretches. Each group's busy time less what it takes at full clock (1.9 for a pair's values, 1.8 for sums, 0.45 for turning, the forecast's figures) is the clock's price. There are 24, 30, 20, 30 and 20 pairs of large blocks in them, and 6, 6, 4, 7.5 and 5 sets of sums and turning (a small block's counts half):

| stretch | values | sums | turning | together | forecast |
|---|---|---|---|---|---|
| `am` | 59.4 - 45.6 = 13.8 | 18.0 - 10.8 = 7.2 | 4.7 - 2.7 = 2.0 | 23.0 | 17.4 |
| `aa`, layer 1 | 86.0 - 57.0 = 29.0 | 20.1 - 10.8 = 9.3 | 6.5 - 2.7 = 3.8 | 42.1 | 17.4 |
| `ab`, layer 1 | 50.8 - 38.0 = 12.8 | 12.7 - 7.2 = 5.5 | 4.3 - 1.8 = 2.5 | 20.8 | 11.6 |
| `aa`, layer 0 | 86.4 - 57.0 = 29.4 | 25.5 - 13.5 = 12.0 | 8.5 - 3.4 = 5.1 | 46.5 | 21.8 |
| `ab`, layer 0 | 50.5 - 38.0 = 12.5 | 13.5 - 9.0 = 4.5 | 4.6 - 2.3 = 2.3 | 19.3 | 14.5 |

Together 152 us instead of 83: values 97.5, sums 38.5, turning 15.7. The forecast priced the values of 57 pairs at 83 and the other two at nothing. Scores and pieces at the lower level are not in this price.

These 152 us are not all new: read in the same way, the values before the change (84.5 us in `aa`, layer 1) already cost 65 us above 1.9 a pair. The forecast measured from the old blocks as they were, with their low clock, and so does its sum. The windows say how much can be new: by their lengths and clocks some 290 us of the five stretches were at the lower level before and some 420 after, and half of the 130 more, 65 us, is the most that half the clock can have added (an estimate). At least some 100 of the 164 us are waiting and work that would be there at full clock too. In `am` the values behind the sums took 1.92 us in four of six blocks before and over 3.3 in all six after; in `aa`, layer 1, they took over 3.2 in all six even before.

The same reading gives 88 us for e4. Its stretches are 154 us shorter than those of the kernel after, so the clock accounts for 64 of these and the additions' own place for 90; the forecast had 83 and 89.7. Two things were left out of the likeliest case. The lower level lasts longer than the values: it covers the sums (3.3 us each in `aa`, where 1.8 was taken) and still holds when the values begin. And in `aa` the values of plain pairs are slow too (3.23 us in the timeline's first pair): twelve pairs at the 3.68 of the timeline would make 21.4 of the 29.0, so at least the rest is theirs.

With a price of 152 the rest of the 164 is 12 us, not 28. The durations taken for full clock explain part of it. Measured at a granted clock of 1.00 (`am` of e11 and e12), a pair's values take 1.94 us, one-column sums 1.95 and turning 0.65, all longer than the forecast's 1.9, 1.8 and 0.45. With these the clock's price is 137 and the rest 27. So the +28 came out right with these three terms some 15 us too small, and others as much too large; which, stays open, and that part of the agreement is luck.

So what happened is the "worse clock" rival in kind: sums at the lower level and plain pairs' values. Its 5225 is 18 us above the measured 5207, and the likeliest case's 5145 is 62 below. It was given 0.13 and named the mechanism of the 62 us. It should have weighed more: [rows 5] shows one stretch at the lower level and not the next, and nothing in it says that the level comes back there.

**"The clock stays up" is refuted.** The Trainium skill ("TensorE: Matmul & The Clock Gate", Loop structure matters more than you think) has VectorE's copies between groups of matmuls leave PE warm, in a loop whose next matmuls follow at once. Here PE waits 1.65 us for VectorE, and in 25 of 26 blocks the 1.2 GHz level began within 4.8 us of that wait's start; the trace decides against carrying the rule over to pauses of this kind. Not every slack stretch has it: before, 4317.5 to 4320.9 had PE busy for 2.36 of 3.4 us, as little as [rows 5], and the next was granted 1.00. The level also falls without an addition between pieces (e4's sums at 4298.59 took 3.55 us).

**"Faster" is refuted for this order and holds for another.** The additions cost little or nothing where an odd step's values cover them. With that alone (e4) the kernel is level with the one before; with the sums behind the values too it is 41 us faster (e6), and 89 in e11. Forecast for this rival was 4924, and none of these runs reaches it. The change put the additions where nothing covers them.

**"No change" fell.** Spreading does make pairs shorter, but the late row (e7, +52) outweighs it in the old kernel (e1, +32).

**GpSimd's seventh addition** was put at nothing, and e12 bears that out (8 us the other way). Inside a stage it did not come late: VectorE starts the merging addition 0.12 us after the reduction ahead of it. At a stage's end the addition does wait for GpSimd, and PE for it: 7.4 us at the end of `aa`, layer 1, and 5.5 before the change.

Left open: what sets the spread of single runs (48 us between the lowest and the highest of e4's ten), what e11's columns do where they follow the values, and why `aa` of layer 0 takes 248 us in e11 and e12 and 238 in e8.

## What to carry to other kernels

An instruction inserted on an engine is free only if nobody waits at that moment for what stands behind it in the queue: look at which handoffs stand behind it, not at the engine's busy share (DVE had 155 us less work here, and the kernel took 171 us longer). Place it where the consumer of those handoffs has long work of its own; one step's difference was worth 164 us. And price what follows a stall at the clock that the trace grants behind such stalls, for everything up to where the trace shows the level rising again (10.2 us in the block above), short matmuls too.

## What the runs showed of the hardware

- Sixteen passes with 128x128 weights and one column take 1.95 us at full clock (e6) and 3.54 at the lower level (the kernel after); with 64 columns 2.0 at full clock (e11: 12.0 for six). So 64 columns instead of one add 0.05 us to sixteen passes.
- Eight passes of values take 1.94 us at full clock (e11's `am`: 46.5 for 24) and 3.68 at the lower level, which lasted 10.2 us from the wait for VectorE to the end of the values.
- A VectorE addition of two 128x1024 operands from SBUF takes 1.23 us alone and 2.25 beside GpSimd's, and GpSimd's two take 5.66 instead of two of 2.36. In the block above GpSimd's first began at 4370.34; if VectorE's waited for its end (4372.70) and then ran 1.23, it would end at 4373.93, seen 4373.80; GpSimd's second would then end at 4376.29 at the latest, seen 4376.00. Each waits for the other's whole instruction. The Trainium skill says so ("SBUF — State Buffer", SBUF: two separate sides: the pair of ports of the two engines is held for the full instruction), and the trace agrees within 0.3 us.
- Order alone, with every engine's instructions the same in number: e4 and e6 are 164 and 214 us faster than the kernel after, while DVE's busy time in `aa`, layer 1, is 113.98 us after and 112.45 in e6.
